# Two-block transformer kernel: k and v turned and scaled earlier in the delta solve, k's totals moved, the first FFN units scaled in pairs

## The reference, cut to what matters

```
h = rms_norm(x, norm_pre_mix)
mix = hybrid_mixer(h)            # attention and a gated delta rule
x = x + rms_norm(mix, norm_post_mix)
f = conv_glu_ffn(rms_norm(x, norm_pre_ffn))
x = x + rms_norm(f, norm_post_ffn)

# gated delta rule, chunks of 64 tokens, 4 heads, k and v 128 wide
k = k * rsqrt(sum(k * k) + EPS)
T = solve(A + eye)               # A strictly lower triangular, 64x64
u = T @ (v * beta);  w = T @ (k * beta * exp(g))
k_dec = k * exp(g_last - g)

# conv_glu_ffn: depthwise conv of 3 taps over time, two halves
u = conv(h @ ffn_w_in) + bias;  gate, up = split(u)
f = (gelu(gate) * up) @ ffn_w_out
```

## Time and profile before

| | |
|---|---|
| median of 3 runs | 2760.77 us (2760.47, 2760.77, 2763.85) |
| the profiled execution, its own time | 2765.85 us |
| its span, first to last instruction | 2764.1 us |
| PE busy | 2685.1 us (97%) |
| DVE, ACT, POOL busy | 1098.6, 1102.5, 1211.5 us (40%, 40%, 44%) |
| PE in the chain that ended last | 87% |
| granted clock over the span | 0.990 |

### The profile page before, as it was taken

How to read it: one execution, slowest core, us unless ns; L and a number is a source line. 1 busy time by engine, 2 the same in 40 slices (tenths; PEclk the granted TensorE clock), 3 DMA queues, 4 the chain that set the end, 5 groups by cost and what they waited for, 6 DMA issues and landing times.

```text
span 2764.1 us, 42821 instructions
## 1 busy us (share of the span) xinstructions
PE 2685.1 (97%) x15208; PEld 2112.3 (76%) x15208; DVE 1098.6 (40%) x2260; ACT 1102.5 (40%) x1871; POOL 1211.5 (44%) x630
## 2 busy tenths in 40 slices
PE   9999999999999999999999999999999999999997
PEld 7767777888877677788887666788888666788886
DVE  4455454441154553644402586510113586510112
ACT  4454254443345533544434235532333235532331
POOL 3323235555433232355544452464653452364653
PEclk9999999999999999999999999999999999999998
DMA  3211023333322100233232221133332221133332
GB/s 136 77 54 40 9 77 91 99 93 105 106 71 69 54 25 24 78 97 96 94 106 92 71 69 47 62 99 99 92 98 84 71 69 47 61 97 94 99 93 97
DMA packets 62867, 217.16 MB, mean 79 GB/s; under 512 B 6576, under 2 KB 6704, under 8 KB 62480
## 3 DMA queue, kind: packets, MB, share of 16 engines
q1 hardware_dynamic: 62416, 214.28, 24.7%
q0 software_dynamic: 320, 1.12, 0.2%
HBM read 213.28 MB, written 2.10 MB: 78 GB/s over the span
## 4 chain that ended last, share of the span: by engine, by line
PE 87%; DVE 5%; ACT 2%; issue 2%; DVEq 2%; POOL 1%; DMA 0%; ACTq 0%; SPq 0%; POOLq 0%
PE bank L1961 61%; PE bank L2337 3%; PE bank L2011 3%; PE bank L2190 2%; PE bank L2191 2%; PE bank L2192 2%; PE bank L2023 1%; PE bank L2222 1%; PE bank L2234 1%; PE bank L2245 1%; PE bank L2127 1%; PE bank L1995 1%; PE bank L2356 1%; DVE mT L1786 1%; PE bank L1988 1%
## 5 line engine op out<-in xcount | busy, mean ns | idle before, releaser
L788 POOL TENSOR_TENSOR wL<-raw,wH 128x1024 fp32r<-128x1024 f32 x371 | 893.1, 2408 | 1085.5 <-ACT wH L977 1085.4
L1961 PE MATMUL bank<-hH,wH 128*128 128x512 f32 x1680 | 679.8, 405 | 7.0 <-DVE mT L1786 4.2
L1961 PE MATMUL bank<-hL,wH 128*128 128x512 f32 x1680 | 657.9, 392 | 0.0
L1961 PE MATMUL bank<-hH,wL 128*128 128x512 f32 x1680 | 657.5, 391 | 0.0
L977 ACT ACTIVATE wH<-raw 128x1024 fp32r<-128x1024 f32 x371 | 392.2, 1057 | 531.1 <-PE bank L1961 490.8
L1961 PEld LDWEIGHTS bank<-hH,wH 128*128 128x128 f32 x1680 | 317.1, 189 | 102.4 <-issue 28.8
L1961 PEld LDWEIGHTS bank<-hH,wL 128*128 128x128 f32 x1680 | 317.3, 189 | 67.5 <-issue 6.0
L1961 PEld LDWEIGHTS bank<-hL,wH 128*128 128x128 f32 x1680 | 316.9, 189 | 67.8
L1961 PE MATMUL bank<-hidH,wH 128*128 128x512 f32 x864 | 336.7, 390 | 0.0
L1961 PE MATMUL bank<-hidH,wL 128*128 128x512 f32 x864 | 336.2, 389 | 0.0
L1961 PE MATMUL bank<-hidL,wH 128*128 128x512 f32 x864 | 336.1, 389 | 0.0
(11 more groups left out here) (378 smaller groups left out, 3629.9 us busy)
## 6 DMA issues: line engine op xcount, KB each, us to landing
raw<-w_dram SPq DMA_DIRECT2D x398, 512.0 KB, 3.5
x<-x_dram SPq DMA_DIRECT2D x4, 512.0 KB, 9.6
out_dram<-x SPq DMA_DIRECT2D x1, 2048.0 KB, 6.3
const<-const_dram SPq DMA_DIRECT2D x1, 1229.0 KB, 13.2
par_next<-par_dram POOLq DMA_DIRECT2D x5, 168.0 KB, 3.5
qkT<-pos_dram POOLq DMA_DIRECT2D x1, 256.0 KB, 7.3
const<-const_dram SPq DMA_DIRECT2D x1, 131.0 KB, 2.2
```

Source lines behind the costliest of these rows:

```text
L788: pool.tensor_tensor(wL[:, s, :], raw[:, s, :], wH[:, s, :].bitcast(F32), ALU.subtract).then_inc(w_lo.sem, 1)
L1961: mm = pe.matmul((out or ACC[bk])[:, :], wt[:, c:c + P], rhs, start=first and k == 0 and j == 0, stop=last and k == tiles - 1 and j == 2)
```

## The change

Four edits. (1) `SOLVE` orders the steps of the solve as 0 to 15, 19, 16, 17, 20, 18, 21, 22. Step 19 on DVE now waits until POOL has made the last level from `ab`, step 20 until step 17 has read `eb`. (2) k's totals (`"total"`) stand behind six products of gate head 0 and `delta_small`. (3) In the first two FFN pairs DVE scales both units before the taps (`both=True`). (4) In these pairs ACT writes both units' lag-0 taps before it makes weights or the gelu (`late=True`, now for both).

More of the change, by code:

```diff
@@ L1282, in hidden_pair @@
                     i2 = i * 2 + q + 18
+                    def shifted(s):
+                        act.wait_ge(acc_scaled.sem, acc_scaled.at(w, i * 4 + 2 * q + s + 13))
+                        act.activation(mT1[:, 2 * q + s, :], banks[s][:, :], ACT.Identity,
+                                       bias=prmd(w, "fbias", i * 4 + 2 * q + s),
+                                       scale=prmd(w, "fconv", i * 12 + 6 * q + 3 * s + 2)).then_inc(glu_in.sem, 1)
                     for s in range(2):
@@ L1287, in hidden_pair @@
                                 next_high(w, i2 + more, s)
[L1288 to L1291, removed]
+                        if s == 0 or not late:
+                            shifted(s)
+                        if s == 0 and late:
+                            shifted(1)
                         for s_, more in units if late else ():
@@ L1775, in _, with hidden_pair, scaled @@
                 dve.wait_ge(rstd_ready.sem, rstd_ready.at(w, 2))
-                def hidden_pair(i, q, banks=ACC):
-                    for s in range(2):
-                        buf = mT1[:, 2 * q + s, :]
+                def hidden_pair(i, q, banks=ACC, both=False):
+                    def scaled(s):
                         dve.wait_ge(unit_done.sem, unit_done.at(w, i * 4 + 37 + 2 * q + s))
@@ L1783, in hidden_pair @@
                                           ALU.mult).then_inc(acc_scaled.sem, 1)
+                    for s in range(2):
+                        buf = mT1[:, 2 * q + s, :]
+                        if s == 0 or not both:
+                            scaled(s)
+                        if s == 0 and both:
+                            scaled(1)
                         dve.wait_ge(glu_in.sem, glu_in.at(w, i * 4 + 2 * q + s + 1))
```

## The result

| | before | after |
|---|---|---|
| median, 19 runs each | 2763.56 us | 2769.46 us |
| ratio of the runs, 95% interval | | 1.0020 (1.0012 to 1.0027) |
| the profiled execution, its own time | 2765.85 us | 2765.85 us |
| its span | 2764.1 us | 2764.1 us |

The change costs 3.3 to 7.5 us by the interval: slower, where I had forecast 4.4 us less. The two profiled executions took equally long by chance: this one of before is high among its runs, the one of after low. So the traces tell where time went, and the medians how much it is.

The account below looks back on a forecast made before the run. PE, busy 97% of the span, was taken to bound the kernel. FFN -6.9, solves +2.8 and totals -0.3 made -4.4 from the median 2760.77, giving 2756.4 us; the 8-in-10 range was 2751.5 to 2761.5.

Parts of the forecast that it names:

- FFN, -6.9: FFN of block one: PE's stall for tap additions and most slow clock behind it vanish; -6.9 us, bounds -7.5 and -4.3.
- the first clash: FFN: the first `piece` meets POOL's low part and ends 0.55 us after it, at no cost.
- Four fifths for the spell: FFN: slow clock behind the stall, 1.6 us a layer, counted at four fifths as 2.6 us gained.
- Solve, +2.8: Solves: waits for banks cost +0.2 us a layer with tiles 0 and 1, +1.2 with tiles 2 and 3; bounds 0 and +4.
- I take one spell again: 0: Solves: one slow-clock spell before and again after, so no difference; bounds -1.6 and +4.8 us.
- rival 2: Solves: the new waits bring a slow spell into each of four, three more; +0.4 us, 2761.2 us; chance 0.14.
- Totals, -0.3: k's totals moved behind gate head 0: one switch between matmul forms falls away; -0.3 us, bounds 0 and -0.6.
- The 1.36 us before the first spread: Gate head 0: ACT's rsqrt waits for its end, which doesn't move, so this wait of 1.36 us stays.
- -6.9 + 2.8 - 0.3: Whole kernel: FFN, solve and totals terms summed to -4.4 us.
- Everything else that the edits touch runs beside PE: Whole kernel: apart from PE's waits for FFN tap additions and the solve's `eb`, touched work doesn't hold PE.
- The third: FFN: second `piece` starts after POOL, from 0.8 us of DVE delay; no gain, 2763.5 us; chance 0.09 with the fourth rival.
- My chance of 0.03 for slower: Whole kernel: slower by over 0.2%, above 2766.3 us, only if the second and third rivals hold together; chance 0.03.

Follow-up runs that it names:

- e1: Kernel before with only the FFN pair edits (both units scaled first, both taps first); 2754.52 us against 2764.29, -9.8.
- e3: Kernel before with only k's totals moved behind six gate products; 2763.30 us against 2764.29, -1.0.
- e5: Kernel before with only the two added DVE waits, steps in the old order; 2771.22 us against 2763.33, +7.9.
- e2: Kernel before with only the new order of the solve's steps and its two waits; 2772.60 us against 2764.29, +8.3.
- e9: Kernel before with the new solve order and its waits, plus 120 drains a layer on DVE; 2766.87 us against 2763.72, +3.1.
- e12: Kernel before with only 8 drains a layer added on DVE in idle time; 2769.70 us against 2763.72, +6.0.
- e6: The whole change plus 120 drains a layer on DVE; 2759.82 us against 2763.33 for the kernel before, -3.5.
- e7: The whole change measured again on another chip; 2765.33 us against 2763.33 for the kernel before, +2.0.
- e4: The change without the new solve order (FFN and totals edits only); 2757.21 us against 2764.29 for the kernel before, -7.1.
- e8: The change with the new solve order in tiles 0 and 1 alone, both waits kept; 2760.25 us against 2763.33 for the kernel before, -3.1.

## Why the prediction was wrong

Its terms had the right mechanisms and, the FFN apart, nearly the right sizes; its sum had a term missing.

- **FFN, -6.9.** Right in its mechanism, too small: e1 measured -9.8 (-14.1 to -6.9), and its trace gives 8.0. The chain came out as written, down to the first clash. Four fifths for the spell were rather many: of the six traces in which the stall is left it follows in both layers in before, e3 and e5, in one in e2 and in none in e9 and e12, 7 of 12.
- **Solve, +2.8.** e9 measured +3.1, so the size is right, but in part for other reasons. With tiles 0 and 1 it was +0.6 in each layer, not +0.2. With tiles 2 and 3 it was +1.2 in waits, as worked out, and about 1.3 on top from a spell behind them in nine of ten solves (after, e2, e6, e7, e9). Against that the spell at step 21 of layer two is gone in all of these. My "I take one spell again: 0" was wrong in both halves and nearly right in sum; rival 2, with a spell in all four solves, saw half of it. The rows that it gives for runs of one kernel that differ, are two layers of one run; runs do differ, by a granted clock of 0.988 to 0.992 in e7.
- **Totals, -0.3.** Not distinguishable: -1.0 in e3, with no difference inside its interval. The 1.36 us before the first spread stays, as forecast.
- **The step that failed** is the sum itself, "-6.9 + 2.8 - 0.3", which has no term for the two waits that edit 1 adds. They are fulfilled or nearly so when DVE arrives (0.13 us a solve in e5), and I took that for no cost. I never asked what 16 more instructions do to the rest of DVE's list, and the sentence "Everything else that the edits touch runs beside PE" closed the book on block two. e5 and e12 give that term: +7.9 and +6.0. With it the sum is +3.9 from e4, e9 and e5 (-7.1 + 3.1 + 7.9), or +0.2 with e1 and e3 in place of e4. The change measured +5.9 on one chip and +2.0 on another, where its interval holds no difference, and its single runs differ by up to 16 us.
- **The rivals.** The third had the mechanism, a DVE operation that comes after POOL instead of before it, and "it decides from" a delay; it looked for it at `piece`, where 0.8 us was in hand. In block two 0.1 us was in hand, in an operation whose 0.36 us I never looked at. My chance of 0.03 for slower was the price of having looked only where the diff is.

The Trainium skill ("SBUF — State Buffer", section "Who interferes with whom") says that a VectorE instruction in a two-port mode and GpSimd share a pair of ports, that the first to issue holds it for its whole length and the other blocks fully, and that tensor_scalar can enter such a mode. For DVE the mask step agrees: behind POOL it takes 2.58 (POOL 2.37) and ends 0.22 after it. For POOL it agrees in part: with DVE in front by 0.1 us the two overlap by 0.26, and POOL takes 2.50, only 0.13 more. With DVE 5 ns behind and still quick POOL takes 2.60, 0.23 more.

```profile
1676.84 2.60 POOL L791 TENSOR_TENSOR wL<-raw,wH 128x1024 fp32r<-128x1024 f32 x1 [9.50 <-ACT wH L980]
1676.84 0.36 DVE L1856 TENSOR_SCALAR bias<-bias 128x384 f32<-128x384 f32 x1
```

**What stays open.** That the position of DVE's list moves the mask step is shown (e5, e6, e12). How a pause of 0.35 us that comes 2.6 us earlier becomes 0.1 us against POOL is only read from the rows, though they read alike in both layers. In before DVE is held at 1673.86, comes later to its next steps, and goes on at once:

```profile
1676.54 0.16 DVE L1551 RECIPROCAL st<-st 128x1 f32<-128x1 f32 x1
1676.68 0.06 DVE L1541 MEMSET st<- 128x1 f32 x1
```

In e5 the pause falls into 1671.13 to 1671.54, where DVE has slack; it then comes earlier, waits 0.10 longer for PE ahead of the same step, and is by that 0.10 later than ACT and POOL, whose pace was set before:

```profile
1671.13 0.29 DVE L1542 CUSTOM_DVE_ANT_0 sc<-bank,bias 128x128 f32<-128x128 f32 x1
1671.54 0.08 DVE L1542 DVE_READ_ACCUMULATOR2_ANT st<- 128x1 f32 x1
...
1676.82 0.16 DVE L1551 RECIPROCAL st<-st 128x1 f32<-128x1 f32 x1
1677.06 0.06 DVE L1541 MEMSET st<- 128x1 f32 x1
```

Other lengths than 0, 8 and 128 instructions more a layer weren't tried, nor a mask step that can't meet POOL. e6 (-3.5) agrees with e4 and e9 (-7.1 + 3.1 = -4.0), but not with e1, e3 and e9 (-7.7); e1 has five runs and an interval of 7 us, so it may be that one that is off. And what brings a spell or keeps it away, in places that no edit touches, is open.

## What to carry to other kernels

In a kernel that is tuned to tenths of a microsecond, an instruction added to one engine's list moves that engine's pauses for all that follows, in places that the diff doesn't touch. So before a change is judged, compare the traces outside it as well, list the pairs of VectorE and GpSimd operations that start within 0.1 us of each other, and repeat the measurement with the old code and as many empty instructions. A change that loses may be a good one in a bad position: here the same edits went from +2.0 to -3.5 by position alone, and to -10.4 with two half products moved to where the new wait is, a good part of it by fewer spells. So count the spells of each trace too before a difference of a few microseconds is put down to an edit.

## What was not expected of the hardware

- DVE's pauses of 0.35 us, 128 instructions apart. The Trainium skill ("Runtime: NRT & Kernel Launch", section "Instruction fetch mechanics") has instructions fetched in blocks of 256 and the cost of a crossing as mostly hidden. Here the gaps stand 128 apart, and they are not hidden where DVE is in a chain. That they are fetches is my reading, and the DMA records of the trace bear it out: in before a packet of 8192 bytes of the kind `instruction` starts 0.2 to 0.9 us behind each of nine such places of DVE's list in block two (2483 to 2995 and 3475 to 3859). At seven of the nine the gap shows.
- The order of the two engines is settled within a few nanoseconds: with DVE 5 ns behind POOL nothing was lost, three times of three (after, e8 twice); with 8 to 14 ns it was 2.2 us, nine times of nine (after, and twice each e2, e5, e7, e12).
- A stall of 2.6 us inside block two brought a spell at 1.2 GHz behind it in both layers of e5, a granted clock of 0.66 in 5 us, which makes 3.5 us of a stall of 2.3. It did so in eight of the nine stalls of this kind, in all but that of after.
